# The first weight slab of a layer loaded and split in two pieces, with tile 0's parts and the first unit between them

## What is computed

```
for l in range(2):
    h = rmsnorm(x, pre_g[l])
    u_a, v_a, g_a, q, k, v, g_b = split(h @ w_in[l])          # 2816 columns
    y = concat(gmlp_group(u_a, v_a, ...) * silu(g_a),
               gqa_axial_attention(q, k, v, ...) * silu(g_b))
    x = x + rmsnorm(y @ w_out[l], post_g[l])
```

## Time and profile before

| | us |
|---|---|
| median of 3 runs | 1059.2 (1057.38 to 1059.92) |
| the profiled execution | 1057.42 |
| its span, first to last instruction | 1055.6 |
| PE busy | 1010.7 (96%) |
| DVE busy | 635.9 (60%) |
| ACT busy | 464.4 (44%) |
| POOL busy | 249.3 (24%) |
| mean granted TensorE clock | 0.996 |

### The profile page before, as it was taken

One profiled execution on the slowest core, in us unless ns is written; L12 is line 12 of the kernel. 1 busy time (PEld: TensorE's weight loads), 2 busy tenths in 40 slices (PEclk: granted clock), 3 DMA queues, 4 the chain that ended last, 5 costly groups with the idle time before them and its releaser, 6 DMA issues.

```text
span 1055.6 us, 13875 instructions
## 1 busy us (share of the span) xinstructions
PE 1010.7 (96%) x5127; PEld 846.1 (80%) x5127; DVE 635.9 (60%) x942; ACT 464.4 (44%) x819; POOL 249.3 (24%) x168
## 2 busy tenths in 40 slices
PE   5999999899999999899999999999999889999996
PEld 4988888687888888687788889887787768888885
DVE  5777677818677677818336576498368983213203
ACT  4445545325445555425356676323465651222211
POOL 2216000002216000002332031134223433223241
PEclk9999999999999999999999999999999999999999
DMA  7423001231433001242322021032210102323311
GB/s 271 132 81 120 21 21 42 79 120 55 145 96 119 21 21 41 80 128 48 120 81 80 1 80 40 5 108 88 80 49 13 40 2 87 111 81 100 120 40 80
DMA packets 66454, 80.46 MB, mean 76 GB/s; under 512 B 5440, under 2 KB 50624, under 8 KB 66384
## 3 DMA queue, kind: packets, MB, share of 16 engines
q1 hardware_dynamic: 64768, 77.17, 23.0%
q10 hardware_dynamic: 1616, 2.36, 0.6%
HBM read 77.42 MB, written 2.10 MB: 75 GB/s over the span
## 4 chain that ended last, share of the span: by engine, by line
PE 53%; issue 28%; DVE 11%; ACT 5%; POOL 2%; DMA 1%; POOLq 0%; SPq 0%; DVEq 0%; ACTq 0%
PE ps L1655 15%; PE ps L1657 14%; PE ps L1656 14%; ACT pw L976 2%; DVE tokw L1502 1%; PE ps L1699 1%; PE ps L1698 1%; PE ps L1697 1%; PE ps L1964 1%; DVE rot L1499 1%; DVE rot L1501 1%; ACT whi L800 1%; DVE small L1577 1%; DMA raw<-in_w_in 1%; PE ps L1970 1%
## 5 line engine op out<-in xcount | busy, mean ns | idle before, releaser
L541 POOL TENSOR_TENSOR wlo<-raw,whi 128x2048 fp32r<-128x2048 f32 (+1 forms) x30 | 132.2, 4408 | 301.9 <-ACT whi L800 301.9
L1655 PE MATMUL ps<-whi,hhi 128*128 128x512 f32 (+1 forms) x320 | 115.9, 362 | 4.6 <-DVE hlo L1040 3.6
L1655 PE MATMUL ps<-hhi,whi 128*128 128x512 f32 x288 | 114.0, 396 | 3.2 <-DVE gate_sw L1537 2.5
L1657 PE MATMUL ps<-whi,hlo 128*128 128x512 f32 (+1 forms) x320 | 114.6, 358 | 0.0
L1656 PE MATMUL ps<-wlo,hhi 128*128 128x512 f32 (+1 forms) x320 | 114.6, 358 | 0.0
L1657 PE MATMUL ps<-hhi,wlo 128*128 128x512 f32 x288 | 113.1, 393 | 0.0
L1656 PE MATMUL ps<-hlo,whi 128*128 128x512 f32 x288 | 113.0, 392 | 0.0
L800 ACT ACTIVATE whi<-raw 128x2048 fp32r<-128x2048 f32 (+1 forms) x35 | 63.6, 1816 | 98.9 <-PE ps L1657 98.8
L1049 DVE TENSOR_TENSOR wlo<-raw,whi 128x2048 fp32r<-128x2048 f32 (+1 forms) x34 | 75.0, 2206 | 42.7 <-ACT whi L591 41.9
L591 ACT ACTIVATE whi<-raw 128x2048 fp32r<-128x2048 f32 (+1 forms) x34 | 61.8, 1816 | 87.1 <-PE ps L1657 84.5
L1697 PE MATMUL ps<-hhi,whi 128*128 128x512 f32 x192 | 78.0, 406 | 0.0
(11 more groups left out here) (298 smaller groups left out, 2346.0 us busy)
## 6 DMA issues: line engine op xcount, KB each, us to landing
raw<-in_w_in SPq DMA_DIRECT2D x45, 1024.0 KB, 5.3
raw<-in_w_out SPq DMA_DIRECT2D x12, 1024.0 KB, 5.0
raw<-in_w_branch_swa SPq DMA_DIRECT2D x4, 1024.0 KB, 5.2
raw<-in_w_in SPq DMA_DIRECT2D x4, 512.0 KB, 3.7
raw<-in_w_branch_sb SPq DMA_DIRECT2D x4, 512.0 KB, 3.4
out<-x SPq DMA_DIRECT2D x4, 512.0 KB, 2.6
x<-in_x ACTq DMA_DIRECT2D x3, 512.0 KB, 6.9
ws<-in_spatial_w SPq DMA_DIRECT2D x2, 512.0 KB, 6.2
```

Source lines behind the costliest of these rows:

```text
L541: pool.tensor_tensor(wlo[s][:, 0:n, :], raw[s][:, 0:n, :], whi[s][:, 0:n, :].bitcast(F32), ALU.subtract).then_inc(slab_split, 1)
L1655: pe.matmul(out_ap, lhsT=lhi(k), rhs=rhi(k), start=first and k == 0, stop=False, skip_group_check=True)
L1657: m = pe.matmul(out_ap, lhsT=llo(k), rhs=rhi(k), start=False, stop=last and k == n - 1, skip_group_check=True)
```

## The change

- `TILE_AT` puts tile 1's transposes ahead of unit (0,1) and no longer ahead of (0,0).
- Slab 0 of every layer is loaded by two DMAs of 256 rows each (two semaphores), and split in two pieces of those rows on ACT (`first_slab_hi`) and on DVE (`first_slab_low`). PE runs unit (0,0) as two halves of six matmuls, each with a wait for its piece.
- On ACT tile 0's parts and the pieces alternate. At the start: piece 0, both halves of tile 0, piece 1, tile 1, slab 1. At the layer ends: piece 0, half 0 of tile 0, piece 1, half 1.
- On DVE at the start: piece 0, half 0 of tile 0, `normalise` of tile 1, piece 1, half 1. At the layer ends `post_norm` comes apart into `post_scale` and `post_add`, and `post_add(2)` goes behind both pieces.
- At the start the load of x tile 2 goes behind the sum of tile 1, and that of x tile 3 (and of the rope table) behind piece 0's high part.

```diff
-TILE_AT = {0: 1, 3: 2, 4: 3}
+TILE_AT = {1: 1, 3: 2, 4: 3}
...
+                    if i == 0:
+                        sp.dma_start(wide(raw[0])[:, 0:2, :], src[:, 0:2, :]).then_inc(first_loaded, 16)
+                        sp.dma_start(wide(raw[0])[:, 2:4, :], src[:, 2:4, :]).then_inc(w_loaded[0], 16)
...
+            def first_slab_hi(l, i, piece):
+
+                if piece == 0:
+                    act.wait_ge(first_loaded, l * 16 + 16 * (i // SLABS) + 16)
+                    act.wait_ge(unit_done, l * UNITS + UNITS_BY_SLAB[SLABS - RING] + UNITS * (i // SLABS - 1) + CREDIT)
+                else:
+                    act.wait_ge(w_loaded[0], l * (8 * SLABS) + 16 * (i // RING) + 16)
+                k = slice(4 * piece, 4 * piece + 4)
+                act.activation(whi[0][:, k, :], raw[0][:, k, :], ACT.Copy).then_inc(whi_done if piece else first_hi, 1)
...
             sum_x(0, 0, 0)
-            load_x(2)
             act.wait_ge(x_loaded[1], 16)
             sum_x(0, 0, 1)
+            load_x(2)
+            first_slab_hi(0, 0, 0)
             load_x(3)
...
-            split_hi(0, 0)
             transposed_x(0, 0, 0)
+            first_slab_hi(0, 0, 1)
             transposed_x(0, 0, 1)
             split_hi(0, 1)
...
                 sum_out(1, 2)
-                split_hi(l, SLABS)
-                transposed_x(l, 1, 0)
+                first_slab_hi(l, SLABS, 0)
+                transposed_x(l, 1, 0, (0,))
+                first_slab_hi(l, SLABS, 1)
+                transposed_x(l, 1, 0, (1,))
                 sum_next(2)
                 sum_out(1, 3)
                 transposed_x(l, 1, 1)
...
             normalise(0, 0, 0)
+            first_slab_low(0, 0, 0)
+            transposed_x(0, 0, 0, (0,))
             normalise(0, 0, 1)
-            slab_low(0, 0)
-            transposed_x(0, 0, 0)
+            first_slab_low(0, 0, 1)
+            transposed_x(0, 0, 0, (1,))
             transposed_x(0, 0, 1)
             slab_low(0, 1)
...
-                post_norm(2)
-                slab_low(l, SLABS)
-                transposed_x(l, 1, 0)
+                post_scale(2)
+                first_slab_low(l, SLABS, 0)
+                transposed_x(l, 1, 0, (0,))
+                first_slab_low(l, SLABS, 1)
+                post_add(2)
+                transposed_x(l, 1, 0, (1,))
                 transposed_x(l, 1, 1)
                 normalise(l, 1, 2)
                 slab_low(l, SLABS + 1)
...
+                    for at_ in (0, 2):
+                        if (i, t) == (0, 0):
+                            pe.wait_ge(*((slab_split, l * SLABS + RING + 1) if at_ else (first_low, l + 1)))
+                        m = product(ps[:, t, :], lambda k: hhi[:, 4 * half + at_ + k, t * P:t * P + P],
+                                    lambda k: hlo[:, 4 * half + at_ + k, t * P:t * P + P], lambda k: hi[:, at_ + k, :],
+                                    lambda k: lo[:, at_ + k, :], 2, first=half == 0 and at_ == 0,
+                                    last=half == 1 and at_ == 2)
```

More of the change, by code:

```diff
@@ L293, in build @@
         slab_asked = sem("slab_asked")
+        first_loaded, first_hi, first_low = sem("first_loaded"), sem("first_hi"), sem("first_low")
         whi_done = sem("whi_done")
@@ L412, in slab @@
                     whole = n >= 0 or i in HALF_K
-                    sp.dma_start(wide(raw[i % RING]) if whole else raw[i % RING][:, :, 0:w], src)\
-                      .then_inc(w_loaded[i % RING], 16)
+                    if i == 0:
+                        sp.dma_start(wide(raw[0])[:, 0:2, :], src[:, 0:2, :]).then_inc(first_loaded, 16)
+                        sp.dma_start(wide(raw[0])[:, 2:4, :], src[:, 2:4, :]).then_inc(w_loaded[0], 16)
+                    else:
+                        sp.dma_start(wide(raw[i % RING]) if whole else raw[i % RING][:, :, 0:w], src)\
+                          .then_inc(w_loaded[i % RING], 16)
                 for i in range(3):
@@ L451, in slab2 @@
                 sp.wait_ge(slab_split, DEPTH * SLABS + j + 1)
-                sp.dma_start(dst, src).then_inc(w_loaded[j % RING], 16)
+                if j == 0:
+                    sp.dma_start(dst[:, 0:2, :], src[:, 0:2, :]).then_inc(first_loaded, 16)
+                    sp.dma_start(dst[:, 2:4, :], src[:, 2:4, :]).then_inc(w_loaded[0], 16)
+                else:
+                    sp.dma_start(dst, src).then_inc(w_loaded[j % RING], 16)
             slab2(0)
@@ L591, in split_hi, with transposed_x @@
                 act.activation(whi[s][:, :, 0:w], raw[s][:, :, 0:w], ACT.Copy).then_inc(whi_done, 1)
-            def transposed_x(l, ahead, t):
-                for half in range(2):
+            def first_slab_hi(l, i, piece):
+                if piece == 0:
+                    act.wait_ge(first_loaded, l * 16 + 16 * (i // SLABS) + 16)
+                    act.wait_ge(unit_done, l * UNITS + UNITS_BY_SLAB[SLABS - RING] + UNITS * (i // SLABS - 1) + CREDIT)
+                else:
+                    act.wait_ge(w_loaded[0], l * (8 * SLABS) + 16 * (i // RING) + 16)
+                k = slice(4 * piece, 4 * piece + 4)
+                act.activation(whi[0][:, k, :], raw[0][:, k, :], ACT.Copy).then_inc(whi_done if piece else first_hi, 1)
+            def transposed_x(l, ahead, t, halves=(0, 1)):
+                for half in halves:
                     act.wait_ge(tr_done, l * 47 + ahead * 47 + 2 * t + half + 1)
@@ L1033, in normalise, with first_slab_low, transposed_x @@
                                          ALU.mult).then_inc(xs_ready, 1)
-            def transposed_x(l, ahead, t):
-                for half in range(2):
+            def first_slab_low(l, i, piece):
+                if piece == 0:
+                    dve.wait_ge(first_hi, l + i // SLABS + 1)
+                else:
+                    dve.wait_ge(whi_done, l * SLABS + i + 1)
+                    dve.wait_ge(slab_split, l * SLABS + RING + i)
+                k = slice(4 * piece, 4 * piece + 4)
+                dve.tensor_tensor(wlo[0][:, k, :], raw[0][:, k, :], whi[0][:, k, :].bitcast(F32),
+                                  ALU.subtract).then_inc(slab_split if piece else first_low, 1)
+            def transposed_x(l, ahead, t, halves=(0, 1)):
+                for half in halves:
                     dve.wait_ge(h_hi, l * 8 + ahead * 8 + 2 * t + half + 1)
@@ L1303, in _, with post_scale @@
                 dve.wait_ge(post_loaded, l * 16 + 16)
-                def post_norm(t):
+                def post_scale(t):
                     if t >= 2:
@@ L1312, in post_norm, with post_add @@
                                              ALU.mult, ALU.mult).then_inc(o_scaled, 1)
+                def post_add(t):
                     dve.wait_ge(o_scaled, l * 4 + t + 1)
                     dve.tensor_tensor(x[:, t, :], x[:, t, :], xo[:, t % 2, :], ALU.add).then_inc(x_back, 1)
-                post_norm(0)
-                post_norm(1)
+                for t in (0, 1):
+                    post_scale(t)
+                    post_add(t)
                 normalise(l, 1, 0)
                 normalise(l, 1, 1)
-                post_norm(2)
-                slab_low(l, SLABS)
-                transposed_x(l, 1, 0)
+                post_scale(2)
[4 more added lines that the diff above has]
+                transposed_x(l, 1, 0, (1,))
                 transposed_x(l, 1, 1)
@@ L1325, in _ @@
                 slab_low(l, SLABS + 1)
-                post_norm(3)
+                post_scale(3)
+                post_add(3)
                 normalise(l, 1, 3)
@@ L1686, in by_token_half @@
                     hi, lo = wide(whi[s]), wide(wlo[s])
-                    product(ps[:, t, :], lambda k: hhi[:, 4 * half + k, t * P:t * P + P],
-                            lambda k: hlo[:, 4 * half + k, t * P:t * P + P], lambda k: hi[:, k, :], lambda k: lo[:, k, :],
-                            4, first=half == 0, last=half == 1).then_inc(unit_done, 1)
+                    m = None
+                    for at_ in (0, 2):
[5 more added lines that the diff above has]
+                                    last=half == 1 and at_ == 2)
+                    m.then_inc(unit_done, 1)
                 def by_column(i, col, bank, part=None):
@@ L1706, in _ @@
                         x_transposed(l, 0, TILE_AT[n])
-                    if t == 0:
+                    if (i, t) == (1, 0):
                         slab_here(i)
@@ L1861, in tokens_half @@
                 hi, lo = wide(whi[s]), wide(wlo[s])
-                product(ps[:, t, :], lambda k: hhi[:, 4 * half + k, tt], lambda k: hlo[:, 4 * half + k, tt],
-                        lambda k: hi[:, k, :], lambda k: lo[:, k, :], 4, first=half == 0, last=half == 1)\
-                    .then_inc(unit_done, 1)
+                m = None
+                for at_ in (0, 2):
+                    if (j, t) == (0, 0):
+                        pe.wait_ge(*((slab_split, DEPTH * SLABS + RING + 1) if at_ else (first_low, DEPTH + 1)))
```

(6 more changed lines are left out.)

## The result

The changed kernel takes 1064.75 us (median of 4 runs, 1064.07 to 1065.3) against 1059.56 for the kernel before (1057.38 to 1060.06) in the same comparison: ratio 1.0054, 95% interval 1.004 to 1.0068. It is slower by 5.2 us. The forecast was 1064.6.

A forecast was written before the change was run, and what follows sets the result against it. PE, busy 96% of the span, bounds the kernel, so only its waits count. Start 1.9 + first layer's end 1.8 + second's 1.7 = 5.4 us, on the median 1059.2, gives 1064.6; range 1059.5 to 1068.

The forecast's parts named there:

- Parts 1 to 4: Layer ends: (0,0) starts 2.25 us earlier, but (0,1) 0.5 later and (1,0) 1.7 and 1.8 us later.
- tile 1's holds: Layer ends: transposes behind (0,0), so (0,1) not before 493.0; then ACT's queue behind post_add(2), so high part at 492.25.
- Part 5: Start of the kernel: (1,0) 1.5 us later from tile 1 and slab 1, plus 0.4 for half rate, +1.9 us.
- the first six at half rate, 0.4 us: Start: first six matmuls of (0,0) run at half pace until 15.75, 0.4 us beyond the wait for piece 1.
- rival B: Start: PE stays slow until it has run (0,0) whole; 1.4 us more, 1066; chance 0.12.
- the other terms: Start: tile 1's open way and slab 1 behind it, (1,0) at 22.6 instead of 21.14, +1.5 us.
- No later wait takes it back: Beyond the changed stretch: ACT, DVE and SP run from PE's units and shift with it, so the 5.4 us stay.
- C: All three places: slab 1 is not late, only (0,1)'s 0.3 + 0.5 + 0.5 remain; 1060.5 us; chance 0.14.
- E: Pieces change nothing, since other waits end at the same times; 1059.2 us; chance 0.04.
- D: Tile 1's way is covered: gain 1.7 at the start, 2.25 at each end, 6.2 in all; 1053 us; chance 0.08.

The follow-up runs named there:

- the run with both put back: Changed kernel with tile 1's transposes back ahead of (0,0) and post_add(2) back right behind post_scale(2): 1058.61 us, ratio 0.9998.
- the run with the move alone: Kernel before with one edit, tile 1's transposes moved behind unit (0,0): 1070.55 us, ratio 1.0104.

## Why the prediction was right, and where it was not

**Parts 1 to 4, the layer ends, hold step by step.** On the scale of before (0,0) was to start at 488.16, tile 1's high part at 492.25, DVE at 492.9, (0,1) at 493.7, slab 1's low part to end at 497.6, (1,0) at 497.65. Measured, less 5.89: 488.17, 492.30, 492.93, 493.68, 497.61, 497.67. Costs 1.7 and 1.8 forecast, 1.72 and 1.87 measured. Every duration had a row of the same operation, most at the same place (the pieces and the handovers from other stretches), and the queue orders were in the code. The prediction named both of tile 1's holds and which is the later one; the runs with one of the two put back show that each is enough.

**Part 5, the start, was mis-sized.** The order, the handovers and the DMA starts were right: piece 0 at 9.99 (10.1), (0,0) at 13.05 (13.0). The two DMA starts of ACT ran beside the copy, at no cost, as these rows of the changed kernel show:

```profile
9.99 1.06 ACT L610 ACTIVATE whi<-raw 128x1024 fp32r<-128x1024 f32 x1 [0.47 <-ACT junk L624]
10.01 0.37 ACTq L629 DMA_DIRECT2D x<-in_x  x1
10.40 0.46 ACTq L639 DMA_DIRECT2D rope<-in_rope  x1
10.96 0.58 ACT L616 ACTIVATE hhi<-ps 128x512 fp32r<-128x512 f32 x1
```

The term that was mis-sized is "the first six at half rate, 0.4 us". Not six but all 12 matmuls were slow, as rival B had it, and (0,0) ended at 18.33 where the full rate behind piece 1 gave 16.7: 1.6. Tile 1's transposes were slow too: from their start to ACT's copy took 1.09 us (18.33 to 19.42) instead of 0.64, another 0.45. So the term measured 2.1 (3.63 less the 1.5 of the other terms) and not 0.4, and (1,0) came 3.63 later where 1.9 was worked out. In the repeat the last matmuls and the transposes ran at full rate; the term measured 1.3 and the loss was 2.78. With PE kept busy and no half rate in (0,0) the loss was 1.89. That it equals the forecast of 1.9 is chance: without the half rate the sum gives 1.5, and in that execution x tile 1 landed 0.24 later (its sum at 8.62 and not 8.38) and held ACT by as much.

**Why the total was right all the same.** The start cost up to 1.7 more than forecast, but the base moved too. The profile of before on which the sum stood had a start at full rate; a second one had not and was 1.56 later at (1,0). So the start's real cost, profile against profile, is between 1.2 (2.78 less 1.56) and 3.6, and the forecast of 1.9 lies inside by luck as much as by working. The ends bring 3.6 of the 5.2 us and are settled; the rest, 1.6, is the start and the scatter behind it, blurred by the clock. How wide the scatter is, the profiled executions tell: the first pair lies 6.65 us apart, the repeats 3.34, the medians 5.2.

**"No later wait takes it back"** holds: PE's lag of 7.75 us stayed 7.75 from 530 to 730. What then shrank it, by 1.6, was the half-rate stretch in one execution and not in the other. In the repeats the lag was 4.58 at the same unit (738.40 and 742.98).

**The rivals.** C (slab 1 in time) and E are out by the waits of 1.0 us for `wlo` at all three places. D, the gain, had named the right condition: tile 1's parts there when (0,0) ends. In the run with both put back that condition is met at the ends, and what follows is 0.3 us, not 2.25: (0,0) itself comes only 0.8 and 1.1 earlier behind the addition, and slab 1's low part becomes the bound at once. So there D's price doesn't follow from its condition; the addition behind the pieces with tile 1 on time was not to be had, since that addition holds tile 1. B happened at the start.

## What to carry to other kernels

Work that is moved behind a unit to let the unit start earlier must be asked what it was hidden beside: here tile 1's way of 2.1 us over two engines had lain beside the very wait that the change removed. Follow the in-order queues to the second and third use, not to the first: the first unit came 2.25 us earlier, and the third came 1.7 later. When two edits each hold the same thing, try all four combinations; here their costs did not add. And before a base profile is trusted to 1 us, take it twice, above all at a start, where TensorE's clock differs between executions.

## What the runs showed of the hardware

- PE's half rate isn't only a matter of the first microseconds. Granted clock 0.50 stood at 16.2 to 19.5 in a second profile of before, after a wait of 2.2 us; at 502.9 to 506.3 in the run with the move alone, after 2.1 us; and near 737 in the first profile of before, after 2.5 us. Each cost 1.5 to 1.6 us. Such a wait doesn't decide it. A wait of 2.3 us ahead of (0,0) in the run of before with extra transposes went without it. The wait of 2.4 to 2.5 us in the third layer stands in all 13 profiles, and a half-rate stretch follows it in nine: in all four of the kernel before and its variants, and in five of the nine with the pieces. Neither profile of the changed kernel has it, but two of its variants do, the one with the addition put back and the one with the x loads put back. What decides it isn't shown.
- At the start the clock column is no guide. In the changed kernel it prints 1.00 over 11 matmuls that came 0.43 apart (the row below); only the durations tell the rate there.

```profile
13.50:17.90 4.40, 4.40 (x11) 3.34 (x11) 2.34 (x3) 0.00 (x0) 0.00 (x0) 1.00 0.84 255
```

- Behind the loop's head, where ACT and DVE begin the second layer, ACT came back after 4.4 us in the first profile of before and after 5.8 in the run of before with extra transposes, and PE then waited 0.8 or 1.9 us for slab 2 (1.3 in the repeat of before). The profile names no cause for the 4.4 ("issue") and PE's last matmul for the 5.8; between the two it costs PE 1.1 us, against 1.7 to 1.9 for a layer's end.

```profile
270.49 0.60 ACT L633 ACTIVATE tok<-ps 128x512 f32<-128x512 f32 x1 [4.44 <-issue]
```

```profile
271.86 0.60 ACT L633 ACTIVATE tok<-ps 128x512 f32<-128x512 f32 x1 [5.80 <-PE ps L1657]
```
